# The exchanged halves of rotary positions: copied by DMA in place of a product with a permutation

## The reference

```python
def rotary(x):                      # and rope(x, pos), with given positions
    x1, x2 = x[..., :half], x[..., half:]
    return jnp.concatenate([x1 * cos - x2 * sin, x2 * cos + x1 * sin], axis=-1)
```

## Time and profile before

| | us |
|---|---|
| median of 3 runs | 1985.4 (1984.94 to 1985.54) |
| the profiled execution | 1986.7 |
| its span, first to last instruction | 1984.9 |
| mean granted clock of PE | 0.989 |
| PE busy, of the span | 1924.1 (97%) |
| DVE busy | 1258.7 (63%) |
| ACT busy | 987.4 (50%) |
| POOL busy | 327.9 (17%) |
| share of PE in the chain that ended last | 80% |

### The profile page before, as it was taken

How to read it: one execution, slowest core, us unless ns; L and a number is a source line. 1 busy time by engine, 2 the same in 40 slices (tenths; PEclk the granted TensorE clock), 3 DMA queues, 4 the chain that set the end, 5 groups by cost and what they waited for, 6 DMA issues and landing times.

```text
span 1984.9 us, 35132 instructions
## 1 busy us (share of the span) xinstructions
PE 1924.1 (97%) x14896; PEld 1820.0 (92%) x14896; DVE 1258.7 (63%) x1641; ACT 987.4 (50%) x1431; POOL 327.9 (17%) x178
## 2 busy tenths in 40 slices
PE   7999999999999999999999999999999999989998
PEld 7989998998899989999988889999999889989997
DVE  6873657665678455767647685576646685566743
ACT  5633455544464534654545444556534444556642
POOL 1060222000014212200001332220001242220000
PEclk9999999999999999999999999999999999999999
DMA  5432344666444324645654443346655433345662
GB/s 207 165 110 96 121 141 152 213 198 200 137 140 137 101 92 138 197 171 172 201 188 139 149 138 113 134 140 202 200 193 180 153 134 117 128 145 181 195 197 101
DMA packets 84539, 308.44 MB, mean 155 GB/s; under 512 B 9376, under 2 KB 9760, under 8 KB 84000
## 3 DMA queue, kind: packets, MB, share of 16 engines
q1 hardware_dynamic: 84384, 306.21, 47.0%
HBM read 305.12 MB, written 1.05 MB: 154 GB/s over the span
## 4 chain that ended last, share of the span: by engine, by line
PE 80%; DVE 13%; ACT 5%; issue 2%; DMA 0%; SPq 0%; ACTq 0%; DVEq 0%
PE bank L1841 78%; DVE wlo L1030 5%; DVE area L1030 4%; DVE area L1036 3%; ACT area L581 2%; ACT whi L587 2%; PE bank L2302 1%; PE bank L2020 1%; DVE xT L1036 0%; DVE B0L L1030 0%; ACT L581 0%; DMA raw<-in_weights 0%; ACT L574 0%; DVE hl L1036 0%; ACT hh L581 0%
## 5 line engine op out<-in xcount | busy, mean ns | idle before, releaser
L1030 DVE TENSOR_TENSOR wlo<-raw,whi 128x1024 fp32r<-128x1024 f32 x512 | 662.0, 1307 | 435.1 <-ACT whi L587 434.5
L1841 PE MATMUL bank<-hh,whi 128*128 128x256 f32 x2928 | 844.4, 288 | 22.8 <-DVE wlo L1030 16.4
L1841 PE MATMUL bank<-hh,wlo 128*128 128x256 f32 x2928 | 820.5, 280 | 0.0
L1841 PE MATMUL bank<-hl,whi 128*128 128x256 f32 x2928 | 820.4, 280 | 0.0
L587 ACT CAST whi<-raw 128x1024 fp32r<-128x1024 f32 x572 | 588.4, 1046 | 360.9 <-PE bank L1841 352.6
L1841 PEld LDWEIGHTS bank<-hh,whi 128*128 128x128 f32 x2928 | 557.4, 190 | 41.7 <-issue 17.9
L1841 PEld LDWEIGHTS bank<-hl,whi 128*128 128x128 f32 x2928 | 558.5, 191 | 6.3 <-issue 6.2
L1841 PEld LDWEIGHTS bank<-hh,wlo 128*128 128x128 f32 x2928 | 558.1, 191 | 0.0
L1624 POOL TENSOR_TENSOR area<-area 128x512 f32<-128x512 f32 (+7 forms) x84 | 133.4, 1595 | 1016.5 <-ACT area L581 671.1
L1841 PE MATMUL bank<-area 128*128 128x128 f32 (+5 forms) x1544 | 200.1, 288 | 5.2 <-issue 3.2
L1624 POOL TENSOR_TENSOR wlo<-raw,whi 128x1024 fp32r<-128x1024 f32 x60 | 149.0, 2483 | 331.8 <-ACT whi L587 331.8
(11 more groups left out here) (126 smaller groups left out, 2046.7 us busy)
## 6 DMA issues: line engine op xcount, KB each, us to landing
raw<-in_weights SPq DMA_DIRECT2D x572, 512.0 KB, 3.9
cst<-in_const SPq DMA_DIRECT2D x1, 1252.0 KB, 10.3
cst<-in_const SPq DMA_DIRECT2D x1, 1088.5 KB, 5.6
xT<-in_x SPq DMA_DIRECT2D x4, 256.0 KB, 5.9
out<-xT SPq DMA_DIRECT2D x1, 1024.0 KB, 3.8
area<-in_lev SPq DMA_DIRECT2D x2, 384.0 KB, 8.2
small<-in_small SPq DMA_DIRECT2D x2, 288.0 KB, 5.1
par<-in_par SPq DMA_DIRECT2D x1, 138.0 KB, 4.1
```

Source lines behind the costliest of these rows:

```text
L1030: return v.tensor_tensor(dst, x, y, op)
L1841: return e.matmul(ps, x, y, start=start, stop=stop, skip_group_check=skip)
```

## The change

The permutation matmuls go. In their place SP issues copies within SBUF that write the exchanged halves to a buffer: for each of the 15 groups four DMAs of 32 partitions (SWAP, two buffers in turn), in the first two layers two DMAs of 64 partitions (TW, in the place of B0H and B0L). The minus sign moves into the sine tables. DVE's sine product reads the buffer instead of a PSUM bank, and in the first two layers is one operation instead of four. ACT's rounding into B0H waits for that product. The groups are placed anew: DVE and POOL handle a group one pair of chunks later, product and addition in one go; groups 4, 5 and 6 stand between the chunks of v2b, 13 and 14 between those of gate0; the step `flushing` goes from the fill of every engine. In DVE the normalisation of the index key moves behind the first chunk of v2a. POOL's order changes as DVE's does. SP issues an exchange behind a given weight fetch, and waits there for the evacuation of the tiles, and for the sine product of the group two before.

```diff
-        R0, R1 = slot(0, 2), slot(2, 2)
+        R0, R1, TW = slot(0, 2), slot(2, 2), slot(28, 2)
...
-        def rope_bank(r):
-            return 5 if (r < 7) == (r % 2 == 0) else 4
+        def swapped(L, r):
+            return s_half[r % 2], 64 * ((L - DEPTH) * ((len(ROPES) + 1 - r % 2) // 2) + r // 2 + 1)
+        def halves(r):
+            n = ROPES[r][1]
+            return SWAP[:, 512 * (r % 2):512 * (r % 2) + n * T]
...
             s.dma_start(LEV, ins["lev"]).then_inc(s_lev[0], 16)
+            def exchange(L, r):
+                m, n, kind = ROPES[r]
+                if kind == "key":
+                    s.wait_ge(*v_rope.at("keyed", L))
+                else:
+                    s.wait_ge(*a_evac.at(kind, L, (m - (11 if kind == "q2b" else 0)) // 2 * 2))
+                if r > 1:
+                    s.wait_ge(*v_rope.at("sin", L, r - 2))
+                for p in range(0, P, 32):
+                    q = p ^ 32
+                    s.dma_start(halves(r)[p:p + 32, :], QF[q:q + 32, m * T:(m + n) * T]).then_inc(s_half[r % 2], 16)
+            def exchange_all(L):
+                s.wait_ge(*a_evac.at("rqk", L, 6))
+                for p in (0, 64):
+                    s.dma_start(TW[p:p + 64, :], RQK[64 - p:128 - p, :]).then_inc(s_swap[L], 16)
+            exchanges = {}
+            for L in (0, 1):
+                exchanges[JOBS["rqk", L].first + 15] = [(exchange_all, L)]
+            for L in (2, 3):
+                a0, b0 = JOBS["q2a", L].first, JOBS["q2b", L].first
+                for r in range(len(ROPES)):
+                    i = a0 + 2 * r + 9 if r < 4 else a0 + 20 if r < 7 else b0 + 2 * (r - 7) + 9
...
                 fetch(i)
+                for f, *which in exchanges.get(i, ()):
+                    f(*which)
                 if i == JOBS["gu", 0].first + 15:
...
                 a.wait_ge(*ready)
+                if name == "wdn":
+                    a.wait_ge(*v_ret.at("rs", L))
...
-                def flushing():
-                    yield
-                fill = chain(project("q2b", L, q_evac("q2b", 11)), flushing(), project("gate0", L),
...
                 v.wait_ge(*v_ret.now())
-                for j in range(4):
-                    v.wait_ge(*e_ret.at("turned", L, j))
-                    tt(v3(pair(R1, j)), v3(bank[j]), wide(SINR, 1, 2), OP.mult).then_inc(*v_ret.up("rs", L, j))
+                v.wait_ge(s_swap[L], 32)
+                tt(v3(R1), v3(TW), wide(SINR, 1, 8), OP.mult).then_inc(*v_ret.up("rs", L))
                 yield 2
                 v.wait_ge(*v_ret.now())
...
-                def rope_add(r):
-                    m, n = ROPES[r][:2]
-                    f = QF[:, m * T:(m + n) * T]
-                    v.wait_ge(*v_rope.at("sin", L, r))
+                def rope(r):
+                    m, n, kind = ROPES[r]
+                    f, t = QF[:, m * T:(m + n) * T], RT[:, 512 * (r % 2):512 * (r % 2) + n * T]
+                    v.wait_ge(*swapped(L, r))
+                    tt(v3(t), v3(halves(r)), wide(SIN if kind == "key" else SINN, 1, n), OP.mult).then_inc(*v_rope.up("sin", L, r))
+                    v.wait_ge(*v_rope.now())
                     v.wait_ge(*g_rope.at("cos", L, r))
-                    tt(f, f, RT[:, 512 * (r % 2):512 * (r % 2) + n * T], OP.add).then_inc(*v_rope.up("add", L, r))
-                def rope(r):
-                    m, n, kind = ROPES[r]
-                    if r not in (0, 7):
-                        rope_add(r - 1)
-                    v.wait_ge(*e_rope.at("turned", L, r))
-                    tt(v3(RT[:, 512 * (r % 2):512 * (r % 2) + n * T]), v3(bank[rope_bank(r)][:, 0:n * T]),
-                       wide(SIN if kind == "key" else SINN, 1, n), OP.mult).then_inc(*v_rope.up("sin", L, r))
+                    tt(f, f, t, OP.add).then_inc(*v_rope.up("add", L, r))
                 def q2a(m0):
                     f = QF[:, 8 * T:9 * T]
-                    if m0 == 10:
-                        v.wait_ge(*a_rope.at("keyunit", L))
-                        stt(f, f, Q("idxk", L), REL[:, 256:512], OP.mult, OP.mult).then_inc(*v_rope.up("keyed", L))
-                        rope(4)
-                        rope(5)
-                    elif m0:
-                        rope(m0 // 2 - 1)
+                    if m0 > 2:
+                        rope(m0 // 2 - 2)
                     if m0 == 8:
                         v.wait_ge(*a_evac.at("q2a", L, 8))
                         tt(f, f, RSB[:, :], OP.mult).then_inc(*v_rope.up("key", L))
+                def key():
+                    f = QF[:, 8 * T:9 * T]
+                    v.wait_ge(*a_rope.at("keyunit", L))
+                    stt(f, f, Q("idxk", L), REL[:, 256:512], OP.mult, OP.mult).then_inc(*v_rope.up("keyed", L))
                 def q2b(m0):
-                    if m0:
-                        rope(6 + m0 // 2)
+                    if m0 > 2:
+                        rope(5 + m0 // 2)
                 rest(project("q2a", L, q2a, tables))
-                rest(project("v2a", L))
-                rope(6)
-                rest(project("v2b", L))
-                rope_add(6)
+                rest(after_step(project("v2a", L), 0, key))
+                rest(after_step(after_step(after_step(project("v2b", L), 0, lambda: rope(4)), 1, lambda: rope(5)), 2, lambda: rope(6)))
...
-                fill = chain(project("q2b", L, q2b), flushing(), project("gate0", L, scaled("gate0", L, GT)),
+                fill = chain(project("q2b", L, q2b),
+                             after_step(after_step(project("gate0", L, scaled("gate0", L, GT)), 0, lambda: rope(13)), 2, lambda: rope(14)),
                              after_step(project("gate1", L, scaled("gate1", L, REL)), 5, lambda: branch_low("wa", L)),
...
-                    g.wait_ge(*e_rope.at("turned", L, r))
+                    g.wait_ge(*swapped(L, r))
                     tt(v3(f), v3(f), wide(COS if kind == "key" else COSN, 1, n), OP.mult).then_inc(*g_rope.up("cos", L, r))
...
             def retention(L):
-                e.wait_ge(*a_evac.at("rqk", L, 6))
-                for j in range(4):
-                    fresh(j, v_ret.at("rs", L, j))
-                    mm(bank[j][:, :], C("rot"), pair(RQK, j), True, True).then_inc(*e_ret.up("turned", L, j))
                 yield 2
...
-                def rope(r):
-                    m, n, kind = ROPES[r]
-                    if kind == "key":
-                        e.wait_ge(*v_rope.at("keyed", L))
-                    else:
-                        e.wait_ge(*a_evac.at(kind, L, (m - (11 if kind == "q2b" else 0)) // 2 * 2))
-                    fresh(rope_bank(r), v_rope.at("sin", L, r))
-                    mm(bank[rope_bank(r)][:, 0:n * T], C2("rot2"), QF[:, m * T:(m + n) * T], True, True).then_inc(*e_rope.up("turned", L, r))
-                def q2a(m0):
+                def key(m0):
                     if m0 == 10:
                         e.wait_ge(*a_rope.at("keysquare", L))
                         fresh(3, a_rope.at("keylog", L))
                         mm(bank[3][:, 0:T], C2("half"), REL[:, 0:T], True, True).then_inc(*e_rope.up("half", L))
-                        rope(4)
-                        rope(5)
-                    elif m0:
-                        rope(m0 // 2 - 1)
-                def q2b(m0):
-                    if m0:
-                        rope(6 + m0 // 2)
-                rest(project("q2a", L, *h, lambda: norm_sum(norm), q2a))
+                rest(project("q2a", L, *h, lambda: norm_sum(norm), key))
                 rest(by_token("v2a", L))
-                rope(6)
                 rest(by_token("v2b", L))
...
-                    rope(14)
-                    yield
-                fill = chain(project("q2b", L, *h, after=q2b), flushing(), project("gate0", L, *h), project("gate1", L, *h), branch("wa", L),
+                fill = chain(project("q2b", L, *h), project("gate0", L, *h), project("gate1", L, *h), branch("wa", L),
                              project("gate2", L, *h), branch("wb", L))
...
-    put("sin", np.tile(np.sin(ang.astype(np.float64)), (2, 1)))
+    put("sin", np.concatenate([-np.sin(ang.astype(np.float64)), np.sin(ang.astype(np.float64))], 0))
...
-    put("inv", np.tile(inv, 4)[:, None])
+    put("inv", np.concatenate([-inv, inv, -inv, inv])[:, None])
```

More of the change, by code:

```diff
@@ L279, in program @@
         s_small = [sem(f"ldsmall{i}") for i in range(DEPTH)]
+        s_half = [sem(f"half{i}") for i in range(2)]
+        s_swap = [sem(f"swap{i}") for i in range(DEPTH)]
         s_par, s_head, s_c1, s_c2, s_pos, s_out = (sem(n) for n in ("ldpar", "ldhead", "ldc1", "ldc2", "ldpos", "out"))
@@ L956, in attend @@
                            bank[3][:, 0:64 * x.nh].rearrange("p (n t) -> p n t", t=128)).then_inc(*a_att.up("OO", L, t))
-                def flushing():
-                    yield
-                fill = chain(project("q2b", L, q_evac("q2b", 11)), flushing(), project("gate0", L),
```

(10 more changed lines are left out.)

36 lines of the change are left out of this document (10 added, 26 removed).

## The result

| | before | changed |
|---|---|---|
| median | 1985.2 us (6 runs, 1982.0 to 1995.6) | 1976.3 us (6 runs, 1972.3 to 1978.0) |
| ratio, 95% interval | | 0.9934 (0.9913 to 0.9956) |
| span of the profiled execution | 1984.9 us | 1974.5 us |
| mean granted clock | 0.989 | 0.985 |

The change is faster, by 0.66%. The forecast was 1955 us with a range from 1941 to 1973: the direction was right, the gain was forecast at 30 and came out at 9, and the median lies 3 us outside the range. Two further comparisons of the same kernel, on other chips, gave 0.9923 (0.9893 to 0.9953) and 0.9924 (0.9894 to 0.9954), so some 15 us. Two of the ten executions in the last of them took far longer (2689 and 6633 us) and are left out of its ratio.

What follows compares the result with a forecast made beforehand. PE was taken as the bound (80% of the span, DVE 13%). Gains of 17.7 us per attention layer, twice 35.4, less 5.0 for retention, gave 30.4 off the median 1985.4: 1955 us, range 1941 to 1973.

Steps and rivals of the forecast that it cites:

- (a): Attention layers: permutation matmuls of 12 wide and 3 narrow groups leave PE's queue; gain 11.4 us per layer.
- (b): Index key: PE no longer waits for the normalised key before group 4; +1.6 us per layer.
- (d): q2b, second query half: becomes bound by DVE, PE waits at chunk 14; -1.3 us per layer, bounds 0 and -3.4.
- (f): First two layers' retention: matmuls leave PE, but POOL holds DVE's sine product; -2.5 us per layer, bounds +2.3 and -6.
- (e): End of attention, wb and wc chunks: fill one step shorter; +4.5 us per layer, bounds 0 and +7.7.
- (c): Flushing step: waits for banks at group 14 and at round 0's values go; +1.5 us per layer.
- (g): SP's queue: each exchange's four issues take 1.7 us and its copies land hidden; 0, bound -3 us per layer.
- DVE takes most of it: Rival, 15%: (e) stays at 0 and (d) at -3.4, less 8 for the retention; 1971 us.
- Everything fits: Rival, 8%: the retention's product is not held and (e) leaves no wait; about 1939 us.

Runs made afterwards that it cites:

- hybrid: Changed kernel with copies for groups 0 to 6 only, groups 7 to 14 by products, no empty step, retention as before: 1972.6 us, 0.9893 of before.
- att_only: Changed kernel with the first two layers' retention as before (permutation products, sine product from PSUM): 1965.7 us, 0.9893 of before.
- both repairs: Changed kernel with retention of the first two layers as before and the sine table of groups 0 to 12 in PSUM: 1964.5 us, 0.9873; again 0.9889.
- psum_sines: Changed kernel with sine tables of the retention and of the attention layers' groups 0 to 12 in PSUM, copies kept: 1966.0 us, 0.9890 of before.
- pool_adds: Kernel with both repairs, each rotary group's add moved from DVE to POOL: 1967.1 us, 0.9873 of before.

## Why the prediction was right or wrong

- **(a)** The matmuls cost what I said: up to the index scores the gain is 6.3 for a forecast of 6.2 with (b), and 4.4 of it comes back with the seven products put back (forecast 4.6). The eight wide products of the second query half, 6.8 us per layer, were taken from PE's queue too, but brought nothing once the empty step was gone: put back, they cost nothing, and with products alone there the ratio is the same (hybrid and att_only, 0.9893). What ate them is (d).
- **(b)** Right in the main. In three of the six layers a wait of 0.5 to 1.0 us is left at that place, for the operand of the product that sums the key's squares, which I had overlooked.
- **(d)** This is the step that failed. I counted one wait of 1.3 at chunk 14, with -3.4 as the bound, and wrote that after chunk 15 "the rounds have slack". They have none. I looked at one chunk, where the stretch to the fourth round has two or three waits per layer: 0.26 and 3.48 in layer 2; 1.33, 1.56 and 2.37 in layer 3, the last at a round's transposes. Over six layers it is 4.9 us of waits and 2.4 of low clock in place of 1.3 of waits. The middle piece lost 5.25 us to the forecast, so (d) was -6.5 and not -1.3. A second thing was wrong, "Its work there is the same": that held for the number of instructions, not their time. The eight products now have both operands in SBUF, as only the additions had, with POOL's products and splits beside them, and DVE came 2.6 us later at chunk 14. I had applied the rule of the Trainium skill ("SBUF — State Buffer", section "SBUF: two separate sides", the exclusive lock of the shared ports) to the retention in (f), with the held rows beside it, and not to the products in q2b, where the same rows spoke; the trace agrees there too (4.59 in place of 1.41). But this second error isn't shown to be what cost time in the attention: with the sine table in PSUM PE's waits for low parts all but go, and the layers still take 275.3 against 274.8.
- Of the layer's shortfall of 6.6 us (17.7 - 11.1), 5.25 is (d), and 1.4 lies behind the fourth round, in (e). Twice 6.6 is 13 us, and (f) adds 1 to 3. The rest of the 21 us between 30 and 9 belongs to no step: the two later comparisons gave 15.
- **(c), (e)** Right: 5.4 measured for 6.0, without any copy. The waits at the second chunk of wb and at the first of wc, forecast 0.7 and 2.4, came out at 0.30 and 2.43, here in the changed kernel, in place of 5.01. Not right was "at full clock": in four of the six layers the clock is low for some 3 us behind the second wait, as in the window below the two rows, and the last piece takes 141.9 to 143.1 us; in the two where it stays at 1.00 the piece takes 140.3 and 140.4, which is the forecast (147.6 - 7.35).

```profile
1286.91 0.36 PE L1859 MATMUL bank<-B0H,whi 128*128 128x256 f32 x1 [0.30 <-DVE area L1067]
1292.31 0.36 PE L1859 MATMUL bank<-B2H,whi 128*128 128x256 f32 x1 [2.43 <-DVE area L1067]
...
1293.50:1296.50 3.00, 3.00 (x16) 3.00 (x16) 1.76 (x2) 0.00 (x0) 0.08 (x1) 0.50 0.35 115
```

- **(f)** The mechanism was right (DVE held by POOL, PE 2.9 later at 239.21, two waits of 3.2 and 3.1), the size too small: 5.7 us over three traces of the changed kernel, 8.1 if all eight traces with its retention are held against the nine with that of before (means of 1056.6 and 1048.5 where layer 2 begins), for a forecast of 5. What I left out of the value taken is the slow clock behind the waits, though it stands in my bound.
- **(g)** Little loss in the changed kernel (0 to 0.7 us at the index scores), and a thinner cover than I gave. Four issues take SP 2.4 us, not 1.7; my 0.37 was a single issue of another shape. The cover is gone when the copies are doubled, and in part with both repairs. The section of the Trainium skill that (g) names for a fixed 2.0 us, "Anatomy of one DMA" in "DMA: Bandwidth & Descriptors", has it for DMAs issued from GpSimd. The copies here are issued from SP, and they landed 3.2 us after their issue (64 KB).
- The rival "DVE takes most of it", with 1971 us and 15%, is what happened, though with (e) kept and (d) at twice its bound. In the rival "Everything fits" the 21 per layer still hold (d) at -1.3 (11.4 + 1.6 + 1.5 - 1.3 + 7.7 = 20.9), so not all bounds are at their best there; with 0 it is 1936 us.

The best of these kernels are those that repair the retention, in either way: 0.9893 (att_only), 0.9890 (psum_sines), 0.9873 and 0.9889 (both repairs), 0.9873 (pool_adds) and 0.9893 (hybrid). They beat the kernel before beyond doubt. Each of their intervals still overlaps at least one of the changed kernel's three, but all six ratios lie below its own (0.9923 to 0.9934). Between themselves they can't be told apart.

## What to carry to other kernels

Work taken off the engine that is last is gained only up to the slack of the next one, and that has to be added up over the whole stretch, not at one chunk: here DVE was 47 of 55 us busy, and eight matmuls vanished into PE's waits for it. When an operand moves from PSUM to SBUF, price the operation again with what runs beside it on POOL; here it cost 6.6 in place of 2.3 us. And what seems part of a change may be had without it: half of the attention layers' gain came from an empty step that could be removed from the old kernel. Two gains that draw on the same slack may not add up: the three parts of this change were priced one by one.

## What the runs showed of the hardware

- At a granted clock of 1.00 the distance between matmuls of 256 columns has two levels, 0.1133 and 0.1178 us. One holds for a whole stage and differs from execution to execution of the same kernel (0.1178 in the MLP of layer 2 in the first trace of the changed kernel, 0.1133 in the second); it makes 6.2 us in an MLP of 177 to 183 us. It is one reason why single runs of the changed kernel spread from 1964 to 1984 us.
- A pause of PE of more than 2 us was mostly followed by a stretch at the lower clock, 1.2 GHz: 0.50 from 1157 to 1163 behind 3.48 us and from 240 to 245 behind 3.11, which cost PE some 3 us each beside the wait, and 0.50 for some 3 us behind waits of 2.37 and 2.43, which cost 1.7 (half of the time that PE worked in the stretch, an estimate). Behind the waits of 1.33 and 1.56 the clock stayed at 1.00, and in two of the six layers behind the wait of 2.34 at wc too.
- Issuing a copy within SBUF takes 0.6 us on SP, and as much on ACT (2.4 us for most groups of four, up to 3.8), where it holds up everything behind it.
